# A hybrid attention and HGRN2 block: the second branch as seven products, and VectorE's order by readiness

## What is computed

```python
h = rmsnorm(x, norm_g)                                   # x is (1024 tokens, 1024)
sb_q, sb_k, sb_v, sb_z, hg_q, hg_f, hg_i, hg_z, gate_logits = split(h @ w_in)
sb_o = sb_attention(sb_q, sb_k, sb_v)                    # stick-breaking, 8 heads of 128
u_sb = (sb_o * silu(sb_z)) @ w_sb_proj
hg_o = rmsnorm(hgrn2_chunked(silu(hg_q), 1 - f, log(f), hg_i), hg_norm_g)   # f from hg_f, 8 heads
u_hg = (hg_o * silu(hg_z)) @ w_hg_proj
gate_sb, gate_hg = split(sigmoid(gate_logits + b_gate))
y = gate_sb * u_sb + gate_hg * u_hg
out = rmsnorm(x + y @ w_out, final_norm_g)
```

## Time and profile before

| what | us |
|---|---|
| median of 3 runs | 1359.86 (1359.74 to 1361.36) |
| the profiled execution's own time | 1358.94 |
| its span | 1357.2 |
| PE busy in the span | 1329.0 (98%) |
| DVE, POOL, ACT busy | 903.1, 709.5, 549.4 |

### The profile page before, as it was taken

The page is one execution under the profiler, slowest core; times in us unless marked ns, Lnnn a source line. Parts: engine busy times, 40 slices in busy tenths (PEclk is TensorE's granted clock), DMA queues, the critical chain, the costliest instruction groups (busy, mean ns, idle before and its releaser), DMA issues.

```text
span 1357.2 us, 22985 instructions
## 1 busy us (share of the span) xinstructions
PE 1329.0 (98%) x8393; PEld 1108.9 (82%) x8393; DVE 903.1 (67%) x1076; ACT 549.4 (40%) x899; POOL 709.5 (52%) x475
## 2 busy tenths in 40 slices
PE   8899999999999999999999999999999999999998
PEld 6788788788878878878888887887887888888886
DVE  5838877877877887787687788778635455645223
ACT  7543355255345335524534533552444431111121
POOL 5655564654665556455466556645578722223310
PEclk9999999999999999999999999999999999999999
DMA  5122111211112211121111211113543485434502
GB/s 187 31 62 65 47 62 32 82 58 46 62 46 73 66 32 62 31 92 56 37 62 46 77 62 31 62 31 118 176 180 133 155 266 191 124 93 132 202 27 98
DMA packets 128168, 118.55 MB, mean 87 GB/s; under 512 B 3920, under 2 KB 110464, under 8 KB 128128
## 3 DMA queue, kind: packets, MB, share of 16 engines
q1 hardware_dynamic: 118816, 92.81, 21.5%
q10 hardware_dynamic: 9312, 25.19, 5.4%
HBM read 88.63 MB, written 29.36 MB: 87 GB/s over the span
## 4 chain that ended last, share of the span: by engine, by line
PE 82%; DVE 7%; issue 5%; POOL 2%; ACT 2%; DMA 1%; ACTq 0%; DVEq 0%; SPq 0%; POOLq 0%
PE banks L1693 44%; PE banks L1986 13%; PE banks L2030 7%; PE banks L1773 5%; PE banks L1751 4%; PE banks L1763 2%; DVE hk L1176 2%; DVE forget L1176 2%; DVE scT L1422 1%; PE banks L1832 1%; PE banks L1737 1%; PE banks L1807 1%; POOL b_lo L631 1%; POOL b_sum L631 1%; PE banks L1834 1%
## 5 line engine op out<-in xcount | busy, mean ns | idle before, releaser
L1693 PE MATMUL banks<-a_hi,b_hi 128*128 128x512 f32 x1064 | 432.7, 407 | 6.4 <-issue 3.8
L1693 PE MATMUL banks<-a_hi,b_lo 128*128 128x512 f32 x1064 | 417.1, 392 | 0.0
L1693 PE MATMUL banks<-a_lo,b_hi 128*128 128x512 f32 x1064 | 415.7, 391 | 0.0
L631 POOL TENSOR_TENSOR b_lo<-w_raw,b_hi 128x512 fp32r<-128x512 f32 x106 | 162.2, 1540 | 231.9 <-ACT b_hi L733 231.9
L631 POOL TENSOR_TENSOR b_lo<-b_sum,b_hi 128x512 fp32r<-128x512 f32 x114 | 167.7, 1471 | 148.2 <-ACT b_hi L733 148.2
L1693 PEld LDWEIGHTS banks<-a_hi,b_hi 128*128 128x128 f32 x1064 | 200.3, 188 | 46.1 <-issue 7.5
L1693 PEld LDWEIGHTS banks<-a_hi,b_lo 128*128 128x128 f32 x1064 | 199.9, 188 | 44.3
L1693 PEld LDWEIGHTS banks<-a_lo,b_hi 128*128 128x128 f32 x1064 | 200.8, 189 | 35.9
L733 ACT ACTIVATE b_hi<-b_sum 128x512 fp32r<-128x512 f32 x114 | 72.0, 632 | 152.5 <-POOL b_sum L631 151.9
L717 POOL TENSOR_TENSOR w_lo<-w_raw,w_hi 128x1024 fp32r<-128x1024 f32 x20 | 54.5, 2730 | 133.5 <-ACT w_hi L733 133.5
L631 POOL TENSOR_TENSOR b_sum<-w_raw 128x512 f32<-128x512 f32 x68 | 102.9, 1513 | 0.0
(11 more groups left out here) (219 smaller groups left out, 2564.8 us busy)
## 6 DMA issues: line engine op xcount, KB each, us to landing
w_raw<-in_w_in SPq DMA_DIRECT2D x72, 512.0 KB, 4.9
gate_d<-gate_out SPq DMA_DIRECT2D x16, 512.0 KB, 4.6
gate_in<-gate_d ACTq DMA_DIRECT2D x32, 256.0 KB, 2.7
x_tok<-in_x SPq DMA_DIRECT2D x8, 512.0 KB, 6.6
z_d<-z_out SPq DMA_DIRECT2D x8, 512.0 KB, 2.7
hz_d<-z_out SPq DMA_DIRECT2D x8, 512.0 KB, 2.7
osb_d<-o_sb SPq DMA_DIRECT2D x8, 512.0 KB, 5.7
ohg_d<-hq SPq DMA_DIRECT2D x8, 512.0 KB, 2.7
```

The costliest lines, as they stand in the source:

```text
L631: return nc.gpsimd.tensor_tensor(dst, a, b, op)
L1693: last = mm(bank, w[:, s, k, :], t[s][:, k, :], start=opens and k == 0 and z == 0, stop=k == QUAD - 1 and z == 2, skip_group_check=not opens)
```

## The change

1. hg's branch is multiplied as four pairs of panels with the seven products of the input projection: 4 x 7 x 12 = 336 matmuls in place of 8 x 48 = 384. The operands of the token side are quarters of hg's gated output, four of them sums or differences: VectorE makes them (`branch_sums`) and their low parts (`branch_low`), ScalarE the high parts (`branch_high`), all beside sb's panels 5 to 7 and the first hg pair. The weights are loaded as pairs into four raw places (two of them new) and split by ScalarE and GpSimd as in the head loop.
2. There is no room for `y_sum` now: each half of sb's gated branch (`ysb_out`) is stored to DRAM (`store_y`), and the whole is loaded again (`load_y`). Each result of a pair is made in a PSUM bank by `y_part`: take the product, multiply by the gate, add the loaded half.
3. `gate_ohg` (two instructions a tile) takes the place of `split_ohg` (four), two tiles beside each of sb's panels 1 to 4.
4. In the head loop HGRN2's steps 6, 7, 8, 9, 11 and 12 come one point later, and VectorE's order changes: c22 before the states, c12 before the output, c21 before any reciprocal; the last two reciprocals and `normalize` of a head come between the scans of the next.
5. In the gate pairs c21 comes before the reciprocals, and of two tiles to be gated the second comes after c22.
6. At the start TensorE waits for each sum of the token side only where a product reads it, no longer for all four before the first pair.
7. All of w_out's panels have their own places, x is loaded again after the last hg product.

The core of the rest of the diff:

```diff
-HG_AT = {1: 0, 3: 1, 6: 3, 9: 4, 12: 5, 14: 6, 17: 7, 19: 8, 21: 9, 23: 11, 26: 12}
+HG_AT = {1: 0, 3: 1, 6: 3, 9: 4, 12: 5, 15: 6, 18: 7, 20: 8, 22: 9, 24: 11, 27: 12}
...
+            def store_y(t):
+                for b in range(2):
+                    sp.wait_ge(gated, 2 * t + b + 1)
+                    sp.dma_start(halfs(y_d[t], b), halfs(ysb_out, b)).then_inc(y_stored[b], 16)
...
+                if e < KT - 1:
+                    sp.wait_ge(panel_done, 2 * KT)
+                else:
+                    sp.wait_ge(product_done, PRODUCTS * (N_PAIRS + N_HG_PAIRS - 1) + P1 + 1)
+                for b in range(2):
+                    sp.wait_ge(y_stored[b], 16 * KT)
...
+            def gate_ohg(i):
+                raw = ohg_tile(OHG_ORDER[i])
+                dve.wait_ge(*ohg_loads(i))
+                tt(raw, raw, both(z_in[i % 2]), ALU.mult).then_inc(ohg_step, 1)
+                dve.wait_ge(ohg_step, 2 * i + 1)
+                dve.wait_ge(ohg_sig_done, i + 1)
+                tt(raw, raw, both(og_sig[i % 2]), ALU.mult).then_inc(ohg_step, 1)
...
+            def branch_low(s):
+                dve.wait_ge(branch_sum, 4)
+                dve.wait_ge(branch_hi, s + 1)
+                tt(flat(og_lo[s]), flat(og_raw[s]), flat(og_hi[s]).bitcast(F32), ALU.subtract).then_inc(branch_ready, 1)
 
...
-
+                    gate_sb(t, b)
+                    if 1 <= t <= KT // 2:
+                        gate_ohg(2 * t - 2 + b)
+                    if t == 5:
+                        for s in ((P5, P6), (P7, P3))[b]:
+                            branch_sums(s)
+                    if t == 6:
+                        for s in ((P1, P6), (P7,))[b]:
+                            branch_low(s)
+                    if t == 7:
+                        for s in ((P5,), (P2, P3))[b]:
...
+            def y_part(i, product, other):
...
+                dve.wait_ge(product_done, PRODUCTS * n + product + 1)
+                if other is None:
+                    dve.wait_ge(gate_loaded[i % 2], 16 * (KT + i // 2 + 1))
+                    tt(bank, pair_bank(n, product), gate_in[:, i % 2, :], ALU.mult).then_inc(first_taken, 1)
+                    dve.wait_ge(first_taken, n + 1)
+                else:
+                    taken = 5 * n + {0: 2, 2: 3, 3: 4}[j]
+                    dve.wait_ge(block_taken, taken)
+                    tt(bank, pair_bank(n, product), other[:, :], ALU.add).then_inc(block_taken, 1)
+                    dve.wait_ge(block_taken, taken + 1)
+                    dve.wait_ge(gate_loaded[i % 2], 16 * (KT + i // 2 + 1))
+                    tt(bank, bank, gate_in[:, i % 2, :], ALU.mult).then_inc(block_gated, 1)
+                    dve.wait_ge(block_gated, 3 * (i // 4) + {0: 1, 2: 2, 3: 3}[j])
+                dve.wait_ge(y_back[e], 16)
+                tt(bank, bank, halfs(y_in[e], half), ALU.add).then_inc(y_made, 1)
...
+            for i in range(N_HG_PAIRS):
+                n = N_PAIRS + i
+                dve.wait_ge(p1_copied, n + 1)
+                take(n, 0, P6 + 1, hg_u2[:, :], pair_bank(n, P6), hg_u3[:, :])
+                if i == 0:
+                    branch_low(P4)
+                else:
+                    y_low(4 * i - 1)
+                take(n, 1, P7 + 1, hg_u3[:, :], pair_bank(n, P7), hg_u2[:, :])
+                y_part(4 * i, P5, hg_u3)
+                y_part(4 * i + 1, P2, None)
+                y_low(4 * i)
+                y_part(4 * i + 2, P3, hg_u2)
+                y_low(4 * i + 1)
+                y_part(4 * i + 3, P4, hg_u2)
+                y_low(4 * i + 2)
+            y_low(4 * N_HG_PAIRS - 1)
...
                     product_waits(n, s)
+                    if isinstance(n, int) and n == 2 and s in SUM_OPERANDS:
+                        pe.wait_ge(s_ready, max(SUM_OPERANDS.index(t) for t in SUM_OPERANDS if t <= s) + 1)
                 last = multiply(pair_bank(parity, s), s, range(2 * (p % 2), 2 * (p % 2) + 2), s <= P5)
...
-            pe.wait_ge(s_ready, 4)
...
+            for i in range(N_HG_PAIRS):
+                n = N_PAIRS + i
+                for s in range(PRODUCTS):
+                    product_waits(n, s)
+                    if i == 0:
+                        pe.wait_ge(branch_ready, s + 1)
+                        if s in (P1, P6):
+                            pe.wait_ge(gated, 2 * KT - 1 + s)
+                    for k in range(QUAD):
+                        for z, (w, t) in enumerate(((hg_b_hi, og_hi), (hg_b_hi, og_lo), (hg_b_lo, og_hi))):
+                            last = mm(pair_bank(n, s), w[s][:, k, :], t[s][:, k, :], start=s <= P5 and k == 0 and z == 0,
+                                      stop=k == QUAD - 1 and z == 2, skip_group_check=s > P5)
+                    last.then_inc(product_done, 1)
...
                 for k in range(KT):
+                    if by_tile and k >= KT - 2:
+                        pe.wait_ge(y_ready, 2 * KT - 2 + (k - (KT - 2)))
                     for z, (y, w) in enumerate(((y_hi, hi), (y_lo, hi), (y_hi, lo))):
```

More of the change, by code:

```diff
@@ new lines, in y_tile @@
+        def y_tile(e, part):
+            return own_tile(e, part) if e < KT - 1 else 64 * KB + part * BLOCK
+        y_hi = tiles("y_hi", lambda e: y_tile(e, 0), F32R)
+        y_lo = tiles("y_lo", lambda e: y_tile(e, 1), F32R)
+        y_in = tiles("y_in", lambda e: y_tile(e, 1))
+        o_hi = place("o_hi", 72 * KB, [4, KT, P], F32R)
+        o_lo = place("o_lo", 32 * KB, [4, KT, P], F32R)
+        wo_hi = place("wo_hi", 88 * KB, [4, KT, P], F32R)
+        wo_lo = place("wo_lo", 48 * KB, [4, KT, P], F32R)
@@ L389, in build @@
         gated = sem("gated")
-        y_part = sem("y_part")
+        y_stored = [sem("y_stored0"), sem("y_stored1")]
+        y_back = [sem(f"y_back{e}") for e in range(KT)]
+        block_gated = sem("block_gated")
+        y_made = sem("y_made")
         y_hi_ready = sem("y_hi_ready")
@@ L1102, in _ @@
                             osb_sigmoid(e)
-                    if p == 7 and not final:
-                        for e in OSB_GATED.get(g, ()):
+                    if p in (7, 10) and not final:
+                        for e in OSB_GATED.get(g, ())[:1] if p == 7 else OSB_GATED.get(g, ())[1:]:
                             osb_high(e)
@@ L1158, in _ @@
+            y_high(4 * N_HG_PAIRS - 1)
+            act.wait_ge(product_done, PRODUCTS * (N_PAIRS + N_HG_PAIRS))
+            for e in range(4, KT):
+                split_panel(out_panel(e), out_weights(e)[0])
             for i in range(NT):
@@ L1601, in _ @@
                 take_u2(n, n)
-                for e in OSB_GATED.get(g, ())[:1 if last_pair else None]:
+                if g == 2:
+                    invert(a, 2)
+                    invert(a, 3)
+                    normalize(a)
+                for e in OSB_GATED.get(g, ())[:1]:
                     osb_gate(e)
@@ L1611, in _ @@
                         osb_multiply(e)
-                for e in OSB_GATED.get(g, ())[:1 if last_pair else None]:
+                    for e in OSB_GATED.get(g, ())[1:]:
+                        osb_gate(e)
+                for e in OSB_GATED.get(g, ())[:1]:
                     osb_low(e)
@@ L1621, in _ @@
                         osb_gate(e)
-                    for e in OSB_GATED[g][1:]:
-                        osb_low(e)
+                for e in OSB_GATED.get(g, ())[1:]:
+                    osb_low(e)
                 dve.wait_ge(gate_stored[0], 16 * g)
```

450 lines of the change are left out of this document (293 added, 157 removed).

## The result

| | before | after |
|---|---|---|
| median of the runs shown, us | 1359.8 (1358.45 to 1361.36, 4 runs) | 1376.78 (1375.86 to 1377.77, 4 runs) |
| profiled execution, us | 1358.94 | 1376.03 |
| its span, us | 1357.2 | 1374.3 |

The ratio of after to before is 1.0125, with a 95% interval from 1.0107 to 1.0142. The forecast was 1347 us with a range from 1333 to 1356, so it was wrong in sign.

A forecast was written before the change was run, and what follows sets the result against it. TensorE, busy for 98% of the span, was taken as the bound, through its matmuls and waits. Terms of -11.4 - 3.8 + 3 - 1.4 - 2.7 + 0.5 + 0.5 + 2.5 gave -12.8 us: 1346.1 profiled, 1347 median, range 1333 to 1356.

The forecast's parts named there:

- The start: Start of the kernel: TensorE's first pair starts earlier and the first turn comes at 73.2 us, -3.8 us.
- VectorE's new order: Head loop: P3 waits for c22 and starts 0.3 to 0.8 us later a head; +0.45 x 7 = +3 us.
- The scans and `normalize`: Head loop: moved `normalize` may add 1.1 us beside GpSimd, row block 2's scans lose up to 0.9 less.
- (c): Rival, slower: late c22 makes the head loop lose more than all else gains; 1365 us, chance 0.04.
- The last head and the gate pairs: After the loop: step 6's wait filled, -1.4 us, and both waits for gate_out gone, -2.7 us.
- Sb's branch: Sb's panels: VectorE's sums fit the half panel of slack, gate halves queue behind hg's output; +0.5 us, bounds 0 and +6.
- Feeding hg's first pair: Hg's first pair: operands and weights arrive nearly in time for TensorE; +0.5 us, bounds 0 and +3.
- The seven products: Hg's branch: 336 matmuls, 76.2 us, replace 384, 87.6 us; -11.4 us if TensorE stays fed.
- From the last pair to the output: First output group waits for the second-last block's low part on VectorE; +2.5 us, bounds 0 and +5.

The follow-up runs named there:

- e9_fed: e7_both with P1's copy before P4's high part, u2 and u3 before P3's and P4's low parts, the squares' first low part before c12: 1338.37 us.
- e8_filler: Kernel after, with six matmuls repeated just ahead of the wait at P3 in seven heads: 1369.18 us, ratio to before 1.0071.
- e3_gate_first: Kernel after, with each gate half's load started before hg's output and z in sb's branch, for panels 2 to 5: 1366.84 us, ratio to before 1.0052.
- e2_order_before: Kernel after, with VectorE's old order in the head loop and the later points of HGRN2's steps kept: 1384.14 us, ratio to before 1.0181.
- e6_first_pair: e3_gate_first, with the last panel's gate halves also loaded and gated earlier, ahead of low parts for hg's first pair: 1367.26 us, ratio to before 1.006.
- e4_before_new_order: Kernel before, with only VectorE's new order in the head loop: 1402.82 us, ratio to before 1.0322.
- e1_loop_before: Kernel after, with VectorE's old order in the head loop and the old points of HGRN2's steps: 1366.32 us, ratio to before 1.0049.
- e5_c22_first: Kernel after, with VectorE taking c22 of the queries' and forget gates' pair before the scans of row block 3: 1354.47 us, ratio to before 0.9964.
- e11_start: Kernel before, with only the new start: 1355.99 us, ratio to before 0.9972.
- e10_before_loop: Kernel before, with only the head loop changed: VectorE's new order, the later steps, and c22 ahead of row block 3's scans: 1355.92 us, ratio 0.9979.
- e7_both: e6_first_pair, with c22 also moved before the scans of row block 3: 1344.91 us, ratio to before 0.9894.

## Why the prediction was wrong, by its own steps

*The start*, -3.8: right in the main, -3.4 in the trace (-3.2 by the timeline) and -3.6 alone on the chip.

*VectorE's new order*, +0.45 us a head: this is the step that failed, though not where it looked. It took P3's wait for c22 as the whole price of the order, at its length. That wait it priced well. It said 1.5 to 2.3 us, and 1.79 came in all seven heads, and the stretch from the first scan to c22's end, for which it said 13.9 us, is 14.1 (297.61 to 311.68). With 0.14 us of spacing and less the 1.45 us won at step 6, that is +0.5 us a head. Two things were missing from the sum:

- *The squares.* The new order also puts `take_output` behind c12. TensorE waits 0.47 us for its low parts, 0.6 with the spacing, in seven heads: 4.3 us. The step followed one consumer of VectorE, P3, and no other. `e9_fed` takes this wait away and the interval falls from 111.8 to 111.1 us.
- *The clock.* The lower clock behind four of the seven waits costs 1.6 us each, three times inside the loop's 13.8 us and once behind it. The step took a wait of 1.31 us at full clock away and put one of 1.79 us in, and counted both at their length. `e8_filler` shows the difference: 7.6 us from filling the wait with work.

7 x 0.5 + 4.3 + 3 x 1.6 = 12.6 us of the 13.8, where the forecast had 3. The rest, 0.1 to 0.2 us a head, is not settled.

*The scans and `normalize`.* The step said that the moved `normalize` would meet GpSimd and lose 1.1 us. It takes 2.23 us in after, in each of the seven heads, against 1.23:

```profile
305.54 2.23 DVE L1398 TENSOR_TENSOR hq<-hq,scT 128x1024 f32<-128x1024 f32 x1
...
311.02 0.66 DVE L1398 TENSOR_TENSOR forget<-banks,u 128x512 f32<-128x512 f32 x1
```

GpSimd works beside both:

```profile
305.40 1.29 POOL L765 TENSOR_TENSOR b_lo<-b_sum,b_hi 128x512 fp32r<-128x512 f32 x1 [1.05 <-ACT b_hi L895]
306.64 2.28 POOL L765 TENSOR_TENSOR b_sum<-w_raw 128x512 f32<-128x512 f32 x1
...
311.11 1.28 POOL L765 TENSOR_TENSOR b_lo<-t,b_hi 128x512 fp32r<-128x512 f32 x1 [0.82 <-ACT b_hi L895]
```

`normalize` takes 1.0 us longer, and c22, with one input in PSUM, has its 0.66 us. That agrees with the Trainium skill, "SBUF — State Buffer", section "Who interferes with whom". The mechanism was there, and it was part of the 14.1 us. The scans of row block 2 gave nearly as much back, as the step had allowed for (0.36 and 1.83 us in after, 1.51 and 1.60 before). So the prediction's price of the moved instruction didn't come. Nor was its sum right: 1.1 us in seven heads on top of 1346.1 is 1353.8, not "1350 or a little more".

*The rivals.* (c) gave the mechanism of a slower kernel, a loop that loses more than all else gains, and the trace has 13.8 us for it where (c) asked for 15.8 against the other terms as forecast. With those the kernel would still have been 2 us faster. But the other terms came to +3.3 us, not -15.8, mostly by the two branches. Against the gains that did come the loop was enough: with sb's branch mended (`e3_gate_first`) the kernel is still 7 us slower than before. I had given it 4 in 100, because I took the bound of the step (1.9 us a head) from VectorE's side alone. 13.8 / 7 is 1.97.

*The last head and the gate pairs*, -4.1: the 2.6 us of waits for gate_out became 1.6 in three, not none, and one slow stretch falls here. Without that stretch the part is -1.7.

*Sb's branch*, +0.5 with a bound of +6: measured +9.7. This step failed too. It had the facts, a gate half "queues behind 1 MB of hg's output and would land 8 to 10 us into a panel". It then took the half panel of slack for enough. What it lacked is when the load is *issued*: behind two tiles and two sigmoids on ScalarE, so at 1125.1 and not at 1119.6. Its estimate of the DMA engines came true: "335 GB/s, at the same ratio a full share" in a panel with hg's output, and 350 GB/s at 1.01 in four panels of `e3_gate_first`. But full engines didn't make TensorE wait there; the late issue of one small load did.

*Feeding hg's first pair*, +0.5 with a bound of +3: 1.2 us of waiting at its first product, 3.8 us of idle time in it, and 3.2 us more of busy time (79.4 us instead of 76.2), of which about 2.7 are the lower clock (5.4 us of matmuls at 0.50, from 1202.1 to 1207.5). It checked each product against ScalarE's list, and not the gated halves of the last panel, which stood on VectorE behind two low parts.

*The seven products*, -11.4: right where TensorE is fed. In `e9_fed` the stage is 81.5 us; less the four waits and their spacing, 4.8, that is 76.7, against 76.2 forecast.

*From the last pair to the output*, +2.5: one wait of 0.35 us; the stage is 1.0 us longer.

Taken together, the gains that the forecast named were real where TensorE was fed, and what failed was the list of waits: it lacked the squares, the clock, the gate's late issue and the late gated halves in hg's first pair. The kernel with the late work moved reaches 1344.9 us by three edits of order and 1338.4 with two more.

## What to carry to other kernels

An order of one engine has as many deadlines as it has consumers. When it is changed, go through all of them, not only through the one that the change is about. A small instruction that frees a bank belongs ahead of long ones that nobody awaits; here one line's move was worth 22 us. And a load's landing time begins with its issue: look at what stands before it on the issuing engine, then at the bytes before it in the queues, and at the mean share last: 0.71 over a stage held four panels at 1.01.

## What the runs showed of the hardware

A wait of TensorE can cost more than its length. In the traces of these kernels, behind the start, no wait of up to 1.69 us (seven of 1.64 to 1.69 us in `e2_order_before`) was followed by a lower granted clock. Longer ones were in part, each time by 3.4 us at 1.2 GHz, which cost 1.6 us where TensorE had work all through it:

- waits of 1.79 us for c22: in four of seven heads in after, `e3_gate_first` and `e6_first_pair`, the same heads in all three, and in two of seven in `e4_before_new_order`;
- waits of 2.0 us for z_out (`e2_order_before`): four of seven; of 2.3 us for the squares (`e4_before_new_order`): five of seven; one of 2.7 us for the squares (`e1_loop_before`): no;
- waits of 2.0 to 3.4 us in sb's branch: none of the three in after, but one each in `e1_loop_before` (2.94), `e2_order_before` (2.06), `e5_c22_first` (2.58) and `e8_filler` (3.38);
- waits of 2.2 to 2.3 us for gate_out in the gate pairs: not in before, but in `e11_start`, `e4_before_new_order` and `e10_before_loop`.

Behind or around the waits of 3.7 and 4.6 us in hg's first pair it was 0.50 in every kernel that had one, for 6.8 us in after, `e2_order_before`, `e5_c22_first` and `e7_both` and for 3.4 us in the four others. Filling 1.36 us of the 1.79 with matmuls kept it at 2.4 GHz in all heads (`e8_filler`). Why the same wait is followed by a slow stretch in one head and not in the next, no run here shows.
